# Attention on one core: the softmax division is moved from the probabilities to the head pairs' outputs, and the value product follows its transposes by two tiles

## The reference, cut to what matters

```python
def one_block(qblk):
    sc = jnp.einsum('bqgrd,btgd->bgrqt', qblk, k).astype(jnp.float32) * scale
    p = jax.nn.softmax(sc, axis=-1).astype(v.dtype)
    return jnp.einsum('bgrqt,btgd->bqgrd', p, v)
...
p = jax.nn.softmax(jnp.concatenate([s_loc, s_ctx], axis=-1), axis=-1).astype(v.dtype)
o = (jnp.einsum('bhrnqk,brnkhd->brnqhd', p[..., :kb], vg)
     + jnp.einsum('bhrnqt,bthd->brnqhd', p[..., kb:], v_ctx))
...
o = jnp.concatenate([o_mla, o_na, o_gqa], axis=-1) @ w_out
```

## Time and profile before

| | |
|---|---|
| median of 3 runs (lowest to highest) | 1957.2 us (1952.45 to 1959.02) |
| the profiled execution: its time, its span | 1961.39 us, 1959.6 us |
| busy over the span: PE, PEld, DVE, ACT, POOL | 89%, 85%, 60%, 37%, 11% |
| attention stage, layer 0 (206.0 to 452.4) | 246.4 us |
| attention stage, layer 1 (1145.0 to 1391.4) | 246.4 us |
| mean granted TensorE clock, span | 0.957 |

### The profile page before, as it was taken

The page is one execution under the profiler, slowest core; times in us unless marked ns, Lnnn a source line. Parts: engine busy times, 40 slices in busy tenths (PEclk is TensorE's granted clock), DMA queues, the critical chain, the costliest instruction groups (busy, mean ns, idle before and its releaser), DMA issues.

```text
span 1959.6 us, 29154 instructions
## 1 busy us (share of the span) xinstructions
PE 1746.5 (89%) x11708; PEld 1671.6 (85%) x11708; DVE 1177.4 (60%) x2221; ACT 719.4 (37%) x1377; POOL 223.6 (11%) x242
## 2 busy tenths in 40 slices
PE   4699778888899999999989967888889999999997
PEld 3699667778899999999989966777889999999997
DVE  6998676783676667676552167678454434444334
ACT  2423665672521221122143266567343121211222
POOL 0001524330000000000010052523000000000001
PEclk9999798999899999999989979899989999999998
DMA  9474000004234433433122010000312222112201
GB/s 317 141 230 125 24 1 2 1 23 150 87 121 161 148 107 119 158 120 118 40 71 78 28 39 1 1 2 23 116 58 65 65 86 64 64 64 91 80 21 54
DMA packets 107912, 159.82 MB, mean 82 GB/s; under 512 B 4976, under 2 KB 85680, under 8 KB 107568
## 3 DMA queue, kind: packets, MB, share of 16 engines
q1 hardware_dynamic: 105024, 152.52, 23.4%
q0 software_dynamic: 640, 2.92, 0.5%
q10 hardware_dynamic: 2160, 3.23, 0.5%
HBM read 155.08 MB, written 3.57 MB: 81 GB/s over the span
## 4 chain that ended last, share of the span: by engine, by line
PE 65%; DVE 25%; ACT 6%; issue 3%; POOL 1%; ACTq 1%; POOLq 0%; DVEq 0%
PE ps L584 21%; PE ps L585 20%; PE ps L586 20%; DVE ps L1228 5%; DVE x L1292 5%; DVE gw L1213 4%; DVE pT L1213 2%; DVE negmax L1430 1%; PE ps L791 1%; DVE K L1213 1%; PE ps L648 1%; DVE Q L1324 1%; PE ps L592 1%; DVE V L1213 1%; ACT pT L1118 1%
## 5 line engine op out<-in xcount | busy, mean ns | idle before, releaser
L584 PE MATMUL ps<-hT,gw 128*128 128x320 f32 x1408 | 437.0, 310 | 6.8 <-DVE hT L1213 6.8
L585 PE MATMUL ps<-hT,gw 128*128 128x320 f32 x1408 | 436.5, 310 | 0.0
L586 PE MATMUL ps<-hT,gw 128*128 128x320 f32 x1408 | 436.5, 310 | 0.0
L1292 DVE SCALAR_TENSOR_TENSOR x<-ps,mod,x 128x320 f32<-128x320 f32 (+2 forms) x576 | 207.7, 430 | 135.9 <-PE ps L586 135.6
L584 PEld LDWEIGHTS ps<-hT,gw 128*128 128x128 f32 x1408 | 265.8, 189 | 7.3 <-issue 7.3
L585 PEld LDWEIGHTS ps<-hT,gw 128*128 128x128 f32 x1408 | 265.8, 189 | 0.0
L586 PEld LDWEIGHTS ps<-hT,gw 128*128 128x128 f32 x1408 | 265.6, 189 | 0.0
L1514 DVE TENSOR_TENSOR mm<-sl,ps 128x320 f32<-128x320 f32 x88 | 42.7, 487 | 342.6 <-issue 210.2
L584 PE MATMUL ps<-act,dw 128*128 128x320 f32 x704 | 219.7, 312 | 17.1 <-DVE x L1292 16.7
L585 PE MATMUL ps<-act,dw 128*128 128x320 f32 x704 | 217.5, 309 | 0.0
L586 PE MATMUL ps<-act,dw 128*128 128x320 f32 x704 | 217.5, 309 | 0.0
(11 more groups left out here) (199 smaller groups left out, 3718.6 us busy)
## 6 DMA issues: line engine op xcount, KB each, us to landing
gw_raw<-in_w_gate SPq DMA_DIRECT2D x22, 1024.0 KB, 5.4
gw_raw<-in_w_up SPq DMA_DIRECT2D x22, 1024.0 KB, 8.0
dw_raw<-in_w_down SPq DMA_DIRECT2D x22, 1024.0 KB, 4.9
ada_w<-in_w_adaT SPq DMA_DIRECT2D x42, 512.0 KB, 6.2
ada_wf<-in_w_adaT SPq DMA_DIRECT2D x34, 512.0 KB, 7.4
wi_raw<-in_w_in SPq DMA_DIRECT2D x16, 912.0 KB, 5.6
ada_wq<-in_w_adaT SPq DMA_DIRECT2D x20, 512.0 KB, 4.0
wo_raw<-in_w_out SPq DMA_DIRECT2D x16, 512.0 KB, 4.3
```

What stands on the lines that cost most here:

```text
L584: pe.matmul(dst, lh, rh, start=start, stop=False, skip_group_check=True)
L585: pe.matmul(dst, lh, rl, start=False, stop=False, skip_group_check=True)
L586: return pe.matmul(dst, ll, rh, start=False, stop=stop, skip_group_check=True)
L1292: i = ve.scalar_tensor_tensor(out=x[:, o, c0:c1], in0=ps[:, banks + hf_, s0:s0 + c1 - c0], scalar=mod[:, l, part * KD + o, q:q + 1], in1=x ...
```

## The change

- The probabilities stay as the exponential leaves them. `normaliser`, `norm_unit`, the 80 single reciprocals and the N steps go. The transposes wait for the exponentials instead of the normalisers.
- Once per pair a step RI, in slot 10 (pair + 1) + 1, takes the reciprocal of the pair's ten sums (128x10) on DVE. SP writes them element by element to a scratch row in DRAM, so that query tokens lie in a line, waits for the landing, and reads them back into the tile `rstd` (128x640), each of two heads' 640 numbers repeated over 64 partitions.
- A step OS on DVE multiplies the pair's output in PSUM by `rstd` in place, 512 columns and then 128, before OL and OP copy it. OL now stands behind the T step of its slot.
- The value product trails its transposes by two T steps: `flush(1)` leaves one product pending, and `pT` gets a third buffer (`pT3`, laid over `ada_w`).
- POOL takes over from DVE the low half of V steps and the two multiplications of GZ steps. POOL's scratch for rotation moves from `rstd` to `rope_t`.
- SP loads the first two tiles of `w_out` just ahead of the last pair's two DMAs.

```diff
         if prompt:
-            order += [("TP", k // 10 - 1), ("OL", k // 10 - 1)]
+            order.append(("TP", k // 10 - 1))
+        if n >= 11 and n % 10 == 1:
+            order.append(("RI", n // 10 - 1))
         order += extra[2 * n]
         if 0 <= k < len(trans):
             order.append(trans[k])
         if prompt:
-            order.append(("OP", k // 10 - 1))
...
+            order += [("OS", k // 10 - 1), ("OL", k // 10 - 1), ("OP", k // 10 - 1)]
...
+            def turn_inverse_sums(l, pair):
+                row = turned[l * NP + pair]
+                sp.wait_ge(rinv_ready, l * NP + pair + 1)
+                sp.dma_start(row.rearrange("c q -> q c"), rinv[:, 10 * pair:10 * pair + 10],
+                             allow_slow_non_contiguous=True).then_inc(r_out, 16)
+                sp.wait_ge(r_out, 16 * (l * NP + pair + 1))
+                sp.wait_ge(o_scaled, l * 2 * NP + 2 * pair)
+                heads = bass.AP(tensor=row.tensor, offset=row.offset, ap=[[T, 2], [0, 64], [1, T]])
+                sp.dma_start(rstd[:], heads).then_inc(rT_ready, 16)
...
+                    elif s[0] == "RI":
+                        if s[1] == NP - 1:
+                            first_wo_loads(l)
+                        turn_inverse_sums(l, s[1])
...
-                def flush():
-                    if pending:
-                        pending.pop()()
+                def flush(keep):
+                    while len(pending) > keep:
+                        pending.pop(0)()
...
-                            pe.wait_ge(p_ready, l * normalised("pool", NH) + normalised("pool", g + 1) - 1)
-                            pe.wait_ge(p2_ready, l * normalised("act", NH) + normalised("act", g + 1))
-                            pe.wait_ge(p3_ready, l * NH + g + 1)
+                            pe.wait_ge(exp_done, l * UNITS + 5 * g + 4)
...
-                        flush()
+                        flush(1)
...
-                        if n >= 2:
-                            sc.wait_ge(pv_done, l * TS + n - 1)
+                        if n >= 3:
+                            sc.wait_ge(pv_done, l * TS + n - 2)
...
-                        sc.wait_ge(pv_done, l * TS + T_AT[("TP", s[1])])
+                        sc.wait_ge(o_scaled, l * 2 * NP + 2 * s[1] + 1)
...
-                        reciprocals(ve, l, u)
...
+                    elif s[0] == "RI":
+                        ve.wait_ge(exp_done, l * UNITS + 10 * s[1] + 10)
+                        ve.reciprocal(rinv[:, 10 * s[1]:10 * s[1] + 10], rsum[:, 10 * s[1]:10 * s[1] + 10]).then_inc(rinv_ready, 1)
+                    elif s[0] == "OS":
+                        ve.wait_ge(pv_done, l * TS + T_AT[("TP", s[1])])
+                        ve.wait_ge(rT_ready, 16 * (l * NP + s[1] + 1))
+                        ve.tensor_tensor(ps[:, 6, :], ps[:, 6, :], rstd[:, 0:LAT], ALU.mult).then_inc(o_scaled, 1)
+                        ve.wait_ge(pv_done, l * TS + T_AT[("TP", s[1])] + 1)
+                        ve.tensor_tensor(ps[:, 7, 0:P], ps[:, 7, 0:P], rstd[:, LAT:T], ALU.mult).then_inc(o_scaled, 1)
...
-                        for dst, src, hi in v_sources(g, 1):
-                            i = lo(dst, src, hi)
+                        for dst, src, hi in v_sources(g, 1):
+                            i = po.tensor_tensor(dst, src, hi.bitcast(F32), ALU.subtract)
...
-                        ve.tensor_tensor(zg, zg, stat[:, t, 2:10].unsqueeze(2).broadcast_to([P, 8, 64]), ALU.mult).then_inc(dve_own, 1)
-                        ve.wait_ge(dve_own, l * NT + t + 1)
-                        ve.tensor_tensor(z[:, t, OFF_G:G_V], z[:, t, OFF_G:G_V], g8[:], ALU.mult).then_inc(g_norm, 1)
+                        po.tensor_tensor(zg, zg, stat[:, t, 2:10].unsqueeze(2).broadcast_to([P, 8, 64]), ALU.mult).then_inc(gz_scaled, 1)
+                        po.wait_ge(gz_scaled, l * NT + t + 1)
+                        po.tensor_tensor(z[:, t, OFF_G:G_V], z[:, t, OFF_G:G_V], g8[:], ALU.mult).then_inc(g_norm, 1)
```

More of the change, by code:

```diff
@@ L81, in na_range @@
     return ns[0], ns[-1]
[L84 to L93, removed]
 def key_slot(g):
@@ L185, in last_t_of, with build @@
     return T_AT[("T", g, 4)]
-def build(nc, a, out):
+def build(nc, a, out, turned):
     ctx = ExitStack()
@@ L199, in build @@
         x = sb("x", [P, KD, T])
+        s0 = ExitStack()
+        pT3 = sb("pT3", [P, 2, 512], F32R, s0)
+        rope_t = sb("rope_t", [P, 6 * 32], F32, s0)
+        s0.close()
         ada_w = sb("ada_w", [P, 2, DM])
@@ L445, in slot_users, with pT_at @@
             return [(m, u) for m, u in tiles if ring_of(m, u)[1] % ring_of(m, u)[0] == slot]
+        def pT_at(n, q, c0, c1):
+            return pT3[:, q, c0:c1] if n % 3 == 2 else pT[:, n % 3, q, c0:c1]
         def in_flight(u, lag):
             return ([u - lag] if u >= lag else []) + (list(range(UNITS - lag, UNITS)) if u == UNITS - 1 else [])
[L452 to L479, removed]
         @block.sync
@@ L496, in wi_load, with wo_load, first_wo_loads @@
                              .rearrange("(k p) n -> p k n", p=P)).then_inc(wi_in[c % 2], 16)
+            def wo_load(l, o):
+                sp.dma_start(wo_raw[:, o % 2], a["w_out"][l, :, o * P:(o + 1) * P]
+                             .rearrange("(k p) n -> p k n", p=P)).then_inc(wo_in[o % 2], 16)
+            def first_wo_loads(l):
+                sp.wait_ge(misc_done, l * NM + NM)
+                sp.wait_ge(v_ready, l * NV + NV)
+                sp.wait_ge(kv_out, l * 64 + 64)
+                sp.wait_ge(norm_out, l * 32 + 32)
+                for o in range(2):
+                    wo_load(l, o)
+            def turn_inverse_sums(l, pair):
[7 more added lines that the diff above has]
+                sp.dma_start(rstd[:], heads).then_inc(rT_ready, 16)
             for l in range(DEPTH):
@@ L540, in _ @@
                         sp.dma_start(out["o_gk"][l], z[:, tile, G_K:G_V]).then_inc(norm_out, 16)
[L542 to L558, removed]
+                    elif s[0] == "RI":
+                        if s[1] == NP - 1:
+                            first_wo_loads(l)
+                        turn_inverse_sums(l, s[1])
+                sp.wait_ge(o_ready, l * 2 * NP + 2 * NP)
+                sp.dma_start(gw_raw[:, 0], a["w_gate"][l, :, 0:256].rearrange("(k p) n -> p k n", p=P)).then_inc(gw_in, 16)
+                sp.dma_start(gw_raw[:, 1], a["w_up"][l, :, 0:256].rearrange("(k p) n -> p k n", p=P)).then_inc(gw_in, 16)
+                sp.dma_start(dw_raw[:], a["w_down"][l, 0:256, :].rearrange("(j p) n -> p j n", p=P)).then_inc(dw_in, 16)
+                if l + 1 < DEPTH:
+                    sp.dma_start(silu_f[:], a["cond"].unsqueeze(0).broadcast_to([P, 2, DM])).then_inc(cond_in, 16)
+                for o in range(2, KD):
+                    sp.wait_ge(wo_ready, l * KD + o - 1)
+                    wo_load(l, o)
                 if l + 1 < DEPTH:
@@ L814, in _ @@
                         n = T_AT[s]
-                        pe.wait_ge(p_ready, l * normalised("pool", NH) + normalised("pool", 2 * pair + 2))
+                        pe.wait_ge(exp_done, l * UNITS + 10 * pair + 10)
                         pe.wait_ge(pT_ready, l * TS + n - 1)
@@ L833, in _ @@
                     elif s[0] == "OP":
-                        flush()
+                        flush(1 if T_AT[("TP", s[1])] + 1 < TS else 0)
                     elif s[0] == "M":
```

60 lines of the change are left out of this document (29 added, 31 removed).

## The result

The changed kernel takes 2047.8 us (median of 4 runs, 2045.6 to 2052.5) beside 1956.2 us of the kernel before: the ratio is 1.0473 with a 95% interval of 1.0447 to 1.0499, slower by 92 us. The forecast was 1926 us, with a range up to 1952; 0.10 was the chance given to slower. It went the way of rival B, a round trip through DRAM that is later than the outputs, and 81 us beyond that rival's 1967 us.

A forecast was written before the change was run, and what follows sets the result against it. A loop of PE, ACT and DVE, PE nearest the bound, its idle time to be won: -16 - 4 + 3.5 + 1.1 = -15.4 us a layer, -30.8 in all, giving 1926.4 us; range 1903 to 1952.

The forecast's parts named there:

- rival B: Round trip 15.3 us, late in gqa, na and tail, 20.3 us a layer; 1967 us, kernel slower; chance 0.12.
- the two DMAs: Between RI and OS: write, read and hand-overs take 7.5 us, hidden in every pair and in the tail.
- The write: Sums to DRAM in 1280 pieces of 4 bytes: taken as 3 us, between 1.4 and 6.4.
- The read: Read-back of 320 KB with a repeated source: taken as 3.9 us, between 2.4 and 3.9.
- Rival A: Read-back runs on two engines, 8.3 us, late in three gqa pairs and the tail; 1936 us; chance 0.22.
- The product's trailing: Value product's 23.2 us wait for `pT` mostly covered by trailing by two: -16 us a layer.
- Relief of DVE and ACT: Attention stage: DVE to about 160 us busy, ACT to 149; K, Q and maxima earlier, -4 us a layer.
- the scaling: OS at a pair's end lengthens the path: +3.5 us a layer over seven pairs, +1.1 in the tail.
- POOL: Attention stage: loses over 45.9 us of 93 busy, gets 21; has room, nothing counted for PE waiting.
- C: PE finds its next wait at the transposes or bank 7; -5.2 us a layer, 1947 us; chance 0.12.
- D: Clock holds too, half-clock stretches go: 24 us below the forecast, 1902 us; chance 0.12.

The follow-up runs named there:

- flat_read16: Changed kernel with its read in two DMAs of 64 rows and its write in 128 pieces of 40 bytes, outputs scaled wrongly; 1907.8 us, ratio 0.9761.
- no_dma: Changed kernel without the two DMAs, outputs scaled by a tile of ones, division left out; 1908.7 us, ratio 0.9765.
- before_trail: Kernel before with only the product trailing its transposes by two, third buffer, OL behind the T step; 1915.0 us, ratio 0.9795.

## Why the prediction was wrong

**The step that failed** is the term of the two DMAs, "3 + 3.9 + 0.6 = 7.5 us, hidden in every pair and in the tail". From issue to issue the write took 11.9 us in the pair shown, 10.5 in the mean of SP's waits, and the read 8.8; the trip from the reciprocal to its use was 20.9 us in that pair. DVE waited 123 us where I had none. Undoing both forms (flat_read16) gives the time of the kernel without DMAs to 1 us. The forecast was 121 us too low: this term cost 139, and the rest of the change won 18 more than the sum said.

**The write.** Its upper bound, 6.4 us, was made from the mean cost of a packet, and "small pieces should be cheaper" led below it. As work for the engines they are: in the pair shown it was over within 2 us. The bound left out that a write ends with its landing, and that many small pieces side by side land late. The page of the profile could not show it; no store of the kernel before has two pieces in the same 64 bytes (the shortest are 128 bytes, in `out_o_kr`). The Trainium skill, DMA: Bandwidth & Descriptors, section Specifications, gives 512 bytes as the least transfer for line rate and says that below it the engine reads, modifies and writes. No run here shows a rate or such a step. What the runs show is that the size of a piece does not settle the landing: SP waited 3.4 us for 1280 pieces of 4 bytes 64 bytes apart, 1.3 us for 128 pieces of 40 bytes, and 10.4 for 1280 pieces of 4 bytes side by side.

**The read.** Rival A had it right: 8.3 us on two engines by its sum, 8.8 measured, 3.4 when the outermost dimension was 64. The Trainium skill, DMA: Bandwidth & Descriptors, section Rules for kernel authors, has the rule on the outermost dimension that the prediction names. The trace agrees: the share in the middle of the read is 0.13 of 16 engines, which is two. I had priced it, and then given it 0.22, because no row spoke for or against.

**Rival B** named the mechanism as it was: DVE held at OS, the next maximum behind it, ACT and PE behind that. It was too cheap because both bounds of its sum were, because it had five late pairs a layer where all eight were late, and because it left out the clock. The point at which it decides is given as 14.1 us; by its own terms it is 14.3.

**The product's trailing.** Taken at 16 us a layer of 23.2; alone it brought 41.1 / 2 = 20.5, and its wait fell from 23.2 to 1.3. The mechanism was right, and that the total came near has some luck in it. PE's idle time fell by 12.2 us, less than the 16, since waits came up elsewhere: 2.6 us a layer at the transposes, as I had feared, and some 3 each before steps on bank 7 and before scores. Busy time fell by 8.6, for which this term had nothing.

**Relief of DVE and ACT, and the scaling.** Forecast -4 and +4.6 a layer, about nothing together. Measured together, as the difference of no_dma (ratio 0.9765) and before_trail (0.9795): 0.3% of 1955, 3 us a layer gained, within what the intervals allow. DVE came to 166 us busy for 160 forecast, ACT to 152 for 149. The V and GZ moves alone are 2 to 3 us a layer, if anything. The scaling was priced at +3.5 for the pairs; with trailing by two the waits for `hT` before steps on bank 7 are 8.5 us a layer (1.5 in the kernel with the trailing alone), and with trailing by one there are 17.8 at bank 6: I had put the two edits side by side, and they are not independent. What the scaling costs by itself was not measured.

**POOL** was at 55 us busy, where the prediction's numbers, 93 - 45.9 + 21, give 68; they leave out two smaller forms of its normaliser. In the attention stage no row has PE waiting for POOL.

**Rivals C and D.** C happened in small part, as told under the trailing. Of D, that the clock recovers with the gaps, a part happened where nothing waited on DMAs. The third mla stretch of the kernel before had 0.82, and without DMAs the clock is full from 262.5 us on, up to 421:

```profile
262.50:421.00 158.50, 140.72 (x912) 120.23 (x910) 116.73 (x208) 108.60 (x265) 34.41 (x38) 1.00 0.03 8
```

Over the stage it is 0.93 for 0.92, and PE's busy time 183.5 us for 194.5. Where DVE waited on DMAs, the reverse happened, 0.82.

## What to carry to other kernels

A transfer through DRAM in the middle of a stage costs what its landing costs: count from issue to landing of both ways, and look at how the pieces lie (many side by side in the same 64 bytes) and at the outermost dimension, before looking at bytes. Turn a small tile on the chip first, and write it in whole rows. And try each part of a change alone: here one part, a product issued one step later, brought 41 us, nearly all that the whole change won without its DMAs (45), and the DMAs gave back 139.

## What the runs showed of the hardware that was not expected

- A write of 1280 pieces of 4 bytes from a 128x10 tile to DRAM, neighbouring queries 4 bytes apart: SP waited 10.4 us before it could issue the next DMA. The same pieces 64 bytes apart 3.4, 512 bytes apart 2.7; 640 pieces 4 bytes apart 8.4; 128 pieces of 40 bytes 1.3; 10 rows of 512 bytes 0.9. In the first form the engines' share was 0.00 for 9.5 of 11.9 us.
- 320 KB read with a source of dimensions 2, 64, 640: 8.8 us, with the engines' share at 0.13, two of 16, in its middle; in two DMAs of 64 rows, 3.4 each.
- TensorE's granted clock over a layer's stage was 0.82 with 8 waits of 7.7 us and 0.93 without them, beside 8 us more of PE's busy time on the same matmuls.
